# HGRN and Mamba mixers of a two-layer transformer step: the order of projections and small products on TensorE

## The chip, the cores and the metric

One core of one Trainium2 chip. The metric is the device time in microseconds of one execution of the whole kernel. The engines are TensorE (PE; its weight loads are listed as PEld), VectorE (DVE), ScalarE (ACT), GpSimd (POOL) and SyncE (SP). The profile counts microseconds from the start of its span.

## The reference

The model runs two layers on a prompt of 512 tokens and on 8 sampled tokens with states of their own. Each layer has a feed-forward block, a mixer and another feed-forward block. Only the mixer of the first layer matters here. Its input `h` is projected once, and then two things are computed side by side:

```python
proj = h @ P['w_in_ab']
q_a, f_a, i_a, g_a, z_b, xbc, dt_raw = jnp.split(...)
# HGRN2, 8 heads of 128: S_t = diag(f_t) S_{t-1} + k_t v_t^T,  o_t = S_t^T q_t
log_f = jnp.log(lb + (1 - lb) * jax.nn.sigmoid(fr)); k_a = (1 - lb) * jax.nn.sigmoid(-fr)
o_a, hg_s = hgrn2_chunked(silu(q_a), k_a, i_a, log_f, hg_s0, HG_CHUNK)
o_a = rmsnorm(o_a, hg_norm) * silu(g_a)
# Mamba-2, 16 heads in 4 groups: S_t = exp(dt_t A) S_{t-1} + B_t (dt_t x_t)^T,  y_t = S_t^T C_t
xbc_c = silu(causal_conv4(xbc) + b)
y, ssm_s = ssd_chunked(xh, dt, a_neg, B, C, ssm_s0, SSM_CHUNK)
y = rmsnorm_by_group((y + D * xh) * silu(z_b))
out = concat([o_a, y]) @ P['w_out_ab']
```

## The kernel before, in words

Everything lies transposed, with features on the partitions and 520 tokens (512 and 8) along the free axis. A product with a 1024 x 128 block of weights ("projection") is done in three passes: the high part of the weights by the high part of the input, the bf16 weights by the input's rest, and the weights' rest by the bf16 input. Each pass has 16 matmuls of 260 columns (`product_by_pass`, L940). ACT cuts the high part and the bf16 part (`cut_parts`, L1616, L1617) and DVE cuts the rest (`hgrn_cut` L2381, `ssm_cut` L2371). Two buffers hold the parts, so that projection number g may be cut once number g - 2 is done (`part_done`). When both weights of a load are cut, DVE frees its half of the ring and SP starts the next load.

The stages run one after the other, with fences between them; each engine has its own hand-written program, and semaphores join them. PSUM has eight banks of 512 columns, and each projection takes two of them.

HGRN, one pass of the loop per head: four projections FORGET, QUERY, VALUE, GATE. PE (`head`, L1117) does VALUE into bank 6 and GATE into bank 4 at the head's start, once the head before is done (`h_done`), with the transposes of the values (L1127) ahead of GATE's last pass. Then come the attention blocks of 128 tokens: product 0 within chunks and seven level products (L1152) with decays for distances 64, 32, ... 1, in banks 0 and 1 alternately, each evicted by DVE (L2475 to L2488). The keys are transposed after product 1 (L1133). Then state products (L1159), the broadcast of the 8 sampled values (L1163), the next head's FORGET into bank 2, output products (L1175, L1177), one-column products of the sampled states (L1181), and the next head's QUERY into bank 0 with the sums of squares (L867) after its first pass. ACT (L1829 on) makes the silu of the queries, the exponentials of decays (L1826, L1828, seven L1831), copies the values (VF, L1833; then L1835 to L1837), makes the silu of the gate (L1839), cuts the next FORGET and QUERY, copies the keys (L1847), multiplies the samples' keys and values (L1808), makes the next forget gates (L1801, L1802), cuts VALUE, squares the output, takes the logarithm of the gates (L1814) and the inverse root (L1572, L1574). DVE (L2431 on) cuts GATE's rest, makes decay differences (L2435 to L2442), products with queries and keys (L2445 to L2454), cuts FORGET and QUERY, splits the sampled values into three bf16 parts (L2462 to L2467), evicts the levels (L2482, L2475, L2485), gathers them (L2488), updates the sampled states (L2494) and the chunk states (L2499, L2502), does the next head's gates and its scan (L2422, L2423, L2426), and applies norm and gate (L2509, L2513). POOL loads the sampled states after `h_done` and stores both kinds of states.

Mamba, one pass per group (PE from L1247): six projections, numbers 0 to 3 for x, B, C, which are convolved on DVE (L2563 to L2569) and get a silu on ACT (L1904), and 4 and 5 for the two halves of z (silu L1901, L1908). PE does numbers 2 to 5, then transposes (L1260 to L1264), the broadcast of cumulated decays (L1269), the products of C and B (L1275), the next group's number 0, the state products (L1282, which wait for DVE's weighted values, L2633), ten filling matmuls (L874), the sample broadcast (L1289), output products (L1299, L1301) once DVE has the chunk states (L2647), one-column products (L1306), and the next group's number 1 with the sums. DVE scales the sampled states by L2596 and turns the transposed x into weighted values from L2600 on.

## Time and profile before

| | us |
|---|---|
| median of 3 runs | 3025.14 (3020.88 to 3027.26) |
| the profiled execution, its own time | 3025.36 |
| its span | 3023.8 |
| PE busy | 2807.6 (93%) |
| DVE busy | 1406.4 (47%) |
| ACT busy | 1355.1 (45%) |
| HGRN stage | about 497 to 838 |
| Mamba stage | about 868 to 1119 |

The span is the profiled execution on the core; 1.6 us lie around it. Busy shares are means over stages. A busy PE is not PE at its peak, since matmuls overlap; the clock that a stretch was granted is given as a share of full speed (1.00 is 2.4 GHz, 0.50 is 1.2 GHz).

### The profile page before, as it was taken

How to read it: one execution, taken by the hardware profiler on the slowest of the kernel's cores; microseconds unless marked ns; L12 is line 12 of the kernel's file. 1: busy time of each engine (PE TensorE's matmuls, PEld its weight loads, DVE VectorE, ACT ScalarE, POOL GpSimd, SP SyncE). 2: the span in 40 equal slices, each digit the busy share in tenths (PEclk: the TensorE clock that was granted, in tenths of full speed). 3: DMA queues.
4: the chain of work that ended last, by engine and by line, in shares of the span. 5: the costliest groups of instructions: out<-in, count | busy, mean ns of one | idle time of the engine just before them, and what ended most of it. 6: DMA issues, size and time to landing. Idle time of an engine off the chain costs nothing.

```text
span 3023.8 us, 60783 instructions
## 1 busy us (share of the span) xinstructions
PE 2807.6 (93%) x24504; PEld 2354.1 (78%) x24504; DVE 1406.4 (47%) x2893; ACT 1355.1 (45%) x2099; POOL 45.1 (1%) x78
## 2 busy tenths in 40 slices
PE   6999997887888989999999999999989989999997
PEld 3899885777667868799888899888856557789996
DVE  2444327666657763634425444333433434544433
ACT  3444337666643444634345434344423334544443
POOL 0000000000000000000000000000000000000000
PEclk8999998989999989999999999999999999999998
DMA  6223442121212224222343123432365435322221
GB/s 241 84 97 123 161 148 86 71 85 64 78 68 89 88 94 184 89 83 95 138 177 117 70 97 123 166 143 79 128 187 161 148 112 191 123 74 94 102 96 67
DMA packets 58281, 349.35 MB, mean 116 GB/s; under 512 B 7537, under 2 KB 7874, under 8 KB 28578
## 3 DMA queue, kind: packets, MB, share of 16 engines
q1 hardware_dynamic: 52274, 322.85, 30.0%
q0 software_dynamic: 5872, 24.59, 2.3%
q8 instruction: 98, 1.61, 0.2%
q14 instruction: 37, 0.30, 0.0%
HBM read 334.96 MB, written 12.45 MB: 115 GB/s over the span
## 4 chain that ended last, share of the span: by engine, by line
PE 76%; DVE 8%; ACT 8%; issue 3%; DVEq 2%; DMA 2%; ACTq 0%; PEldq 0%; SPq 0%; POOL 0%; PEld 0%
PE PS L940 54%; PE PS L918 2%; PE PS L954 2%; PE PS L867 2%; PE PS L1436 1%; PE PS L978 1%; PE PS L1418 1%; PE PS L1421 1%; PE PS L874 1%; PE PS L1397 1%; ACT hgrn_w_hi L1616 1%; DMA weight_ring<-in_mla_pairs 1%; PE PS L899 1%; ACT sub_out L1831 1%; PE PS L962 1%
## 5 line engine op out<-in xcount | busy, mean ns | idle before, releaser
L2167 DVE TENSOR_TENSOR w_rest<-weight_ring,w_hi 128x1024 bf16<-128x1024 f32 (+1 forms) x268 | 320.8, 1197 | 857.4 <-ACT w_hi L1616 857.2
L1616 ACT ACTIVATE w_hi<-weight_ring 128x1024 fp32r<-128x1024 f32 (+1 forms) x284 | 294.8, 1038 | 889.1 <-PE PS L940 886.0
L940 PE MATMUL PS<-hid_hi,w_hi 128*128 128x260 f32 x2432 | 326.9, 286 | 0.0
L940 PEld LDWEIGHTS PS<-hid_hi,w_hi 128*128 128x128 f32 x2432 | 299.2, 188 | 2.3
L940 PE MATMUL PS<-hid_rest,w_bf 128*128 128x260 bf16 x2432 | 298.4, 274 | 0.0
L940 PE MATMUL PS<-hid_bf,w_rest 128*128 128x260 bf16 x2432 | 296.7, 274 | 0.0
L1617 ACT ACTIVATE w_bf<-weight_ring 128x1024 bf16<-128x1024 f32 (+1 forms) x284 | 289.7, 1020 | 0.0
L940 PEld LDWEIGHTS PS<-hid_bf,w_rest 128*128 128x128 bf16 x2432 | 235.6, 97 | 36.5
L940 PEld LDWEIGHTS PS<-hid_rest,w_bf 128*128 128x128 bf16 x2432 | 223.9, 97 | 38.6
L940 PE MATMUL PS<-gu_hi,w_hi 128*128 128x260 f32 x1232 | 168.7, 288 | 0.0
L940 PEld LDWEIGHTS PS<-gu_hi,w_hi 128*128 128x128 f32 x1232 | 152.8, 188 | 14.1 <-issue 11.2
L940 PE MATMUL PS<-gu_rest,w_bf 128*128 128x260 bf16 x1232 | 152.3, 274 | 0.0
L940 PE MATMUL PS<-gu_bf,w_rest 128*128 128x260 bf16 x1232 | 151.3, 273 | 0.0
L940 PEld LDWEIGHTS PS<-gu_bf,w_rest 128*128 128x128 bf16 x1232 | 119.1, 97 | 18.6
L940 PE MATMUL PS<-hgrn_in_rest,hgrn_w_bf 128*128 128x260 bf16 x1056 | 133.0, 276 | 0.0
L940 PE MATMUL PS<-hgrn_in_bf,hgrn_w_rest 128*128 128x260 bf16 x1056 | 130.7, 274 | 0.0
L940 PE MATMUL PS<-mixer_in_hi,hgrn_w_hi 128*128 128x260 f32 x864 | 122.7, 297 | 6.3 <-ACT hgrn_w_hi L1616 5.1
L940 PEld LDWEIGHTS PS<-gu_rest,w_bf 128*128 128x128 bf16 x1232 | 112.8, 97 | 19.7
L940 PEld LDWEIGHTS PS<-mixer_in_hi,hgrn_w_hi 128*128 128x128 f32 x864 | 112.3, 198 | 9.7 <-ACT hgrn_w_hi L1616 5.4
L940 PEld LDWEIGHTS PS<-hgrn_in_bf,hgrn_w_rest 128*128 128x128 bf16 x1056 | 102.3, 97 | 16.2
L940 PEld LDWEIGHTS PS<-hgrn_in_rest,hgrn_w_bf 128*128 128x128 bf16 x1056 | 97.5, 98 | 18.7
L874 PE MATMUL PS<-consts 128*128 128x512 bf16 x337 | 86.6, 414 | 2.9 <-DVEq L558 2.9
(487 smaller groups left out, 4471.8 us busy)
## 6 DMA issues: line engine op xcount, KB each, us to landing
weight_ring<-in_ffn_gu SPq DMA_DIRECT2D x88, 1024.0 KB, 4.8
ada_chunks<-in_ada_w SPq DMA_DIRECT2D x40, 1536.0 KB, 6.6
weight_ring<-in_ffn_wd SPq DMA_DIRECT2D x32, 1408.0 KB, 6.0
weight_ring<-in_w_hgrn SPq DMA_DIRECT2D x16, 1024.0 KB, 4.8
weight_ring<-in_ada_w SPq DMA_DIRECT2D x8, 1536.0 KB, 7.2
weight_ring<-in_w_ssm SPq DMA_DIRECT2D x8, 1536.0 KB, 6.9
weight_ring<-in_mla_pairs SPq DMA_DIRECT2D x8, 1536.0 KB, 6.5
weight_ring<-in_w_out_ab SPq DMA_DIRECT2D x8, 1024.0 KB, 7.9
```

Of the source, the lines that this page charges most:

```text
L867: last = pe.matmul(PS[0:rows, bank + hf, 0:HT], weights[k], moving[k][:, hf * HT:(hf + 1) * HT], start=(k == 0), stop=(k == n - 1))
L874: pe.matmul(PS[:, bank, :], STEADY[:, 0:P], STEADY[:, 0:4 * P], start=True, stop=True)
L899: last = pe.matmul(PS[:, bank, 0:HT], w[:, k * P:(k + 1) * P], x[:, k, side(hf)], start=start and w is w_hi, stop=stop and w is w_rest)
L918: last = pe.matmul(PS[:, bank, 0:HT], w[:, k * P:(k + 1) * P], x[:, first + k, side(hf)], start=start and w is w_hi and k == 0, stop=stop ...
L940: last = pe.matmul(PS[:, bank + hf, 0:HT], w[:, k * P:(k + 1) * P], x[:, first + k, hf * HT:(hf + 1) * HT], start=start and w is w_hi and ...
L954: last = pe.matmul(PS[q * QR_:(q + 1) * QR_, 4, 0:3 * P], CS[:, k, :], weights[:, k * 3 * P:(k + 1) * 3 * P], start=(k < 4), stop=(k >= 4))
L962: last = pe.matmul(PS[:, 5, c * NSEQ:(c + 1) * NSEQ], MS[:, c * P:(c + 1) * P], const("fold")[:, 0:NSEQ], start=True, stop=True)
L978: last = pe.matmul(PS[:, 7, 0:HT], ONES, Y[:, c, side(hf)], start=(c == 0), stop=(c == DC - 1))
L1397: last = pe.matmul(PS[:, 4, :], WF[:, first:first + P], CKV[:, k, 0:NP_], start=(k == 0), stop=(k == RC - 1))
L1616: act.activation(hi, src, ACT.Copy).then_inc(w_hi_ready, 1)
L1617: act.activation(bf, src, ACT.Copy).then_inc(w_bf_ready, 1)
L2167: tt(WL_[:, buf, 0:n], W[:, slot, j * DC * P:j * DC * P + n], WH[:, buf, 0:n].bitcast(F32), ALU.subtract).then_inc(w_rest_ready, 1)
```

## The change

In HGRN the next head's four projections are spread over this head: FORGET after the key transposes (which come after all levels), QUERY after the sample broadcast, VALUE with the sums in it and GATE with the value transposes in it after the one-column products. VALUE now uses bank 2. On DVE the evictions of the levels come before the cuts of FORGET and QUERY and the splitting of the sampled values; the state update comes behind the next head's gates, so that the samples' gates and keys are copied first (FS, KS). ACT's program follows. In Mamba the second z half moves behind the products of C and B into bank 4; ACT copies it between the second and third segment exponential and makes its silu later. The diff, cut where "..." stands:

```diff
--- before.py
+++ after.py
@@ -285,6 +285,7 @@
         VM = yar.take(P // 2, rows=NB).bitcast(BF16)
+        FS, KS = yar.take(NB), yar.take(NB)
         S0 = ar.take(NB, P)
@@ -468,6 +469,7 @@
         g_z = sem("g_z")
+        g_zraw = sem("g_zraw")
         g_sel = sem("g_sel")
@@ -682,7 +684,7 @@
         QBANK, QTILE = (6, 2, 0), (0, 2 * 4, 4)
-        XBANK, ZBANK = (4, 2, 0, 6), (2, 0)
+        XBANK, ZBANK = (4, 2, 0, 6), (2, 4)
 
@@ -1115,27 +1117,26 @@
             def hgrn():
-                def project(h, c, bank, between=None, late=False):
-                    product_by_pass(hgrn_group(h, c), bank, c % 2, DC, 0, GHH, GHB, GHL, True, True,
+                def project(h, c, bank, between=None, late=False, ahead=0):
+                    product_by_pass(hgrn_group(h, c) + 4 * ahead, bank, c % 2, DC, 0, GHH, GHB, GHL, True, True,
                                     (GWH, GWB, GWL), between, late).then_inc(part_done, 1)
 
+                def values_and_gate(h, ahead, sums=None):
+
+                    def values_by_token():
+                        pe.wait_ge(h_vf, h + ahead + 1)
+                        for c in range(NCH):
+                            pe.transpose(PS[:, 2, c * P:(c + 1) * P], VF[:, c * CH:(c + 1) * CH], IDENT)
+                        pe.transpose(PS[0:NB, 3, 0:P], VF[:, NP_:T], IDENT).then_inc(h_vt, 1)
+
+                    pe.wait_ge(h_exp, h * 3 + (3 * ahead + 1))
+                    project(h, VALUE, 2, sums, False, ahead)
+                    if ahead:
+                        pe.wait_ge(h_r, h + 1)
+                    project(h, GATE, 4, values_by_token, True, ahead)
+
                 def head(h, more):
 
-                    def values_by_token():
-                        pe.wait_ge(h_vf, h + 1)
-                        for c in range(NCH):
-                            pe.transpose(PS[:, 6, c * P:(c + 1) * P], VF[:, c * CH:(c + 1) * CH], IDENT)
-                        pe.transpose(PS[0:NB, 7, 0:P], VF[:, NP_:T], IDENT).then_inc(h_vt, 1)
-
-                    def keys_by_token():
-                        pe.wait_ge(h_exp, h * 3 + 3)
-                        for c in range(NCH):
-                            last = pe.transpose(PS[:, 4, c * P:(c + 1) * P], KD[:, c * CH:(c + 1) * CH], IDENT)
-                        last.then_inc(h_kt, 1)
-
-                    pe.wait_ge(h_done, h + 1)
-                    project(h, VALUE, 6)
-                    project(h, GATE, 4, values_by_token, True)
                     pe.wait_ge(h_kd, h + 1)
@@ -1152,21 +1153,30 @@
                         last.then_inc(h_p, 1)
-                        if n == 1:
-                            keys_by_token()
+                    pe.wait_ge(h_exp, h * 3 + 3)
+                    for c in range(NCH):
+                        last = pe.transpose(PS[:, 4, c * P:(c + 1) * P], KD[:, c * CH:(c + 1) * CH], IDENT)
+                    last.then_inc(h_kt, 1)
+                    pe.wait_ge(h_v, h + 1)
+                    if more:
+                        project(h, FORGET, 2, None, False, 1)
+                    else:
+                        keep_busy(2, 12)
                     pe.wait_ge(h_kdt, h + 1)
...
                     pe.wait_ge(h_vs, h + 1)
+                    pe.wait_ge(h_done, h + 1)
                     for b in range(NB):
...
                     if more:
-                        project(h + 1, FORGET, 2)
+                        pe.wait_ge(h_ptk, h * 8 + 10)
+                        project(h, QUERY, 0, None, False, 1)
                     else:
-                        keep_busy(2, 30)
+                        keep_busy(2, 24)
                     pe.wait_ge(h_vk, h + 1)
@@ -1187,7 +1197,7 @@
                     if more:
-                        project(h + 1, QUERY, 0, sums)
+                        values_and_gate(h, 1, sums)
                     else:
@@ -1216,6 +1226,7 @@
                 pe.wait_ge(vec_in, 64)
+                values_and_gate(0, 0)
                 with pe.Fori(0, HG - 1) as h:
@@ -1249,9 +1260,8 @@
                     project(g, 3, XBANK[3])
-                    for c in range(2):
-                        pe.wait_ge(g_raw, g * 4 + (c + 2))
-                        project(g, 4 + c, ZBANK[c])
+                    pe.wait_ge(g_raw, g * 4 + 2)
+                    project(g, 4, ZBANK[0])
 
@@ -1264,7 +1274,7 @@
                     pe.wait_ge(g_sel, g + 1)
-                    pe.wait_ge(g_z, g * 2 + 2)
+                    pe.wait_ge(g_z, g * 2 + 1)
                     for j in range(GH):
@@ -1274,8 +1284,10 @@
                     last.then_inc(g_cb, 1)
-                    if more:
-                        pe.wait_ge(g_xd, g + 1)
+                    pe.wait_ge(g_xd, g + 1)
+                    project(g, 5, ZBANK[1])
+                    if more:
+                        pe.wait_ge(g_zraw, g + 1)
                         project(g + 1, 0, XBANK[0])
@@ -1806,7 +1818,7 @@
                         last = act.activation(VK[:, b, :], PS[:, 6 + b // 4, (b % 4) * P:(b % 4 + 1) * P],
-                                              ACT.Identity, scale=KK[:, NP_ + b:NP_ + b + 1])
+                                              ACT.Identity, scale=KS[:, b:b + 1])
                     last.then_inc(h_vk, 1)
@@ -1816,9 +1828,9 @@
                 forget_log(0)
+                cut(0, GATE)
 
                 def head(h, more):
-                    cut(h, GATE)
                     projected(h, QUERY)
@@ -1830,34 +1842,38 @@
                     projected(h, VALUE)
-                    act.activation(two(VF), pair(6), ACT.Copy).then_inc(h_vf, 1)
+                    act.activation(two(VF), pair(2), ACT.Copy).then_inc(h_vf, 1)
+                    if more:
+                        cut(h, FORGET, 1)
+                    else:
+                        ssm_cut(0, 0)
                     act.wait_ge(h_vt, h + 1)
-                    act.activation(VS, PS[0:NB, 7, 0:P], ACT.Copy)
-                    act.activation(V3[0:NB], PS[0:NB, 7, 0:P], ACT.Copy)
-                    act.activation(VV.rearrange("p a b -> p (a b)"), PS[:, 6, :], ACT.Copy).then_inc(h_v, 1)
+                    act.activation(VS, PS[0:NB, 3, 0:P], ACT.Copy)
+                    act.activation(V3[0:NB], PS[0:NB, 3, 0:P], ACT.Copy)
+                    act.activation(VV.rearrange("p a b -> p (a b)"), PS[:, 2, :], ACT.Copy).then_inc(h_v, 1)
                     projected(h, GATE)
+                    act.wait_ge(h_done, h + 1)
                     act.activation(two(GS), pair(4), ACT.Silu).then_inc(h_exp, 1)
                     if more:
-                        cut(h, FORGET, 1)
+                        act.preload_act_table_set("sigmoid_and_others")
                         cut(h, QUERY, 1)
                     else:
-                        ssm_cut(0, 0)
                         ssm_cut(0, 1)
...
                     if more:
-                        act.preload_act_table_set("sigmoid_and_others")
-                    sample_products(h)
-                    if more:
                         forget_gates(h, 1)
                         cut(h, VALUE, 1)
+                    else:
+                        both_tables()
+                    sample_products(h)
+                    if more:
+                        forget_log(h, 1)
                     act.wait_ge(h_o, h * 2 + 2)
...
                     if more:
-                        forget_log(h, 1)
-                    else:
-                        both_tables()
+                        cut(h, GATE, 1)
                     act.wait_ge(h_ss, h + 1)
@@ -1904,15 +1920,11 @@
                         ssm_cut(g, 0, 1)
-                    projected(g, 5)
-                    act.activation(two(GZ[:, 1, :]), pair(ZBANK[1]), ACT.Silu).then_inc(g_z, 1)
                     act.wait_ge(g_tr, g + 1)
...
                         act.activation(CEX[:, j, :], PS[:, j, :], ACT.Exp).then_inc(g_bcx, 1)
-                    if more:
-                        ssm_cut(g, 1, 1)
                     act.wait_ge(g_wl, g + 1)
@@ -1920,6 +1932,13 @@
                         act.activation(SEG[:, j, :], SEG[:, j, :], ACT.Exp).then_inc(g_sege, 1)
+                        if j == 1:
+                            projected(g, 5)
+                            act.activation(two(GZ[:, 1, :]), pair(ZBANK[1]), ACT.Copy).then_inc(g_zraw, 1)
+                    if more:
+                        ssm_cut(g, 1, 1)
+                    act.drain()
+                    act.activation(GZ[:, 1, :], GZ[:, 1, :], ACT.Silu).then_inc(g_z, 1)
                     if more:
@@ -2452,21 +2471,6 @@
                         tt(d[:, :, 0, :], d[:, :, 0, :], k[:, :, 0, :], ALU.mult).then_inc(h_qk, 1)
-                    if more:
-                        cut(h, FORGET, 1)
-                        cut(h, QUERY, 1)
-                    else:
-                        ssm_cut(0, 0)
-                        ssm_cut(0, 1)
-                    dve.wait_ge(h_v, h + 1)
-                    tt(VR, VS, V3[0:NB], ALU.subtract)
-                    dve.drain()
-                    dve.tensor_copy(VM, VR)
-                    dve.drain()
-                    tt(V3[64:64 + NB], VR, VM, ALU.subtract)
-                    dve.tensor_copy(V3[32:32 + NB], VM)
-                    dve.drain().then_inc(h_vs, 1)
-
                     for n in range(1 + len(LEVELS)):
@@ -2487,12 +2491,24 @@
                     dve.drain().then_inc(h_att, 1)
-
-                    dve.wait_ge(s_loaded, h * 16 + 16)
-                    dve.wait_ge(h_vk, h + 1)
-                    for b in range(NB):
-                        last = stt(S0[:, b, :], S0[:, b, :], FG[:, NP_ + b:NP_ + b + 1], VK[:, b, :], ALU.mult, ALU.add)
-                    last.then_inc(s_new, 1)
+                    if more:
+                        cut(h, FORGET, 1)
+                    else:
+                        ssm_cut(0, 0)
+                    dve.wait_ge(h_v, h + 1)
+                    tt(VR, VS, V3[0:NB], ALU.subtract)
+                    dve.drain()
+                    dve.tensor_copy(VM, VR)
+                    dve.drain()
+                    tt(V3[64:64 + NB], VR, VM, ALU.subtract)
+                    dve.tensor_copy(V3[32:32 + NB], VM)
+                    dve.tensor_copy(KS, KK[:, NP_:T])
+                    dve.drain().then_inc(h_vs, 1)
+                    if more:
+                        cut(h, QUERY, 1)
+                    else:
+                        ssm_cut(0, 1)
+
 
@@ -2502,8 +2518,17 @@
                     dve.drain().then_inc(h_s, 1)
-                    if more:
+                    dve.wait_ge(s_loaded, h * 16 + 16)
+                    if more:
+                        dve.tensor_copy(FS, FG[:, NP_:T])
                         forget(h, 1)
+                    else:
+                        dve.tensor_copy(FS, FG[:, NP_:T])
+                        dve.drain()
+                    dve.wait_ge(h_vk, h + 1)
+                    for b in range(NB):
+                        last = stt(S0[:, b, :], S0[:, b, :], FS[:, b:b + 1], VK[:, b, :], ALU.mult, ALU.add)
+                    last.then_inc(s_new, 1)
 
@@ -2661,6 +2686,7 @@
                     dve.drain()
+                    dve.wait_ge(g_z, g * 2 + 2)
                     tt(EV[:, 0:2, :], EV[:, 0:2, :], GZ, ALU.mult)
```

## Rows read from the trace of the kernel before

**Rows 1.** Windows, both stages: us, busy PE, PEld, DVE, ACT, POOL, clock, DMA share, GB/s.

```profile
497.00:838.00 341.00, 277.96 (x3679) 243.71 (x3680) 224.50 (x573) 220.93 (x350) 13.30 (x23) 0.90 0.21 74
868.00:1119.00 251.00, 223.69 (x1694) 187.50 (x1692) 190.29 (x424) 109.93 (x154) 17.09 (x27) 0.93 0.25 89
```

**Rows 2.** Waits, HGRN stage (497 to 838): us in total, times, longest.

```profile
PE PS L1152 <- DVE weight_parts L2482: 43.3, 8, 5.7
...
PE PS L1127 <- ACT arena L1833: 9.9, 8, 1.4
```

**Rows 3.** Timeline, PE in HGRN heads: start, us, engine, line, instructions, idle before.

```profile
534.50 0.65 PE L1175 MATMUL PS<-arena 128*128 128x128 f32 x4
...
746.17 0.68 PE L1175 MATMUL PS<-arena 128*128 128x128 f32 x4 [0.59 <-DVEq L2504]
...
747.80 1.84 PE L1181 MATMUL PS<-arena 128*128 128x1 f32 x16
...
749.51 2.16 PE L940 MATMUL PS<-mixer_in_hi,hgrn_w_hi 128*128 128x260 f32 x16
...
751.51 1.04 PE L867 MATMUL PS<-arena,consts 128*128 128x260 f32 x4
...
755.96 2.17 PE L940 MATMUL PS<-mixer_in_hi,hgrn_w_hi 128*128 128x260 f32 x16
...
761.48 2.17 PE L940 MATMUL PS<-mixer_in_hi,hgrn_w_hi 128*128 128x260 f32 x16
...
776.50 3.75 PE L1152 MATMUL PS<-sub_out 128*32 128x32 f32 x176 [5.44 <-DVE weight_parts L2482]
...
789.04 0.68 PE L1175 MATMUL PS<-arena 128*128 128x128 f32 x4 [0.60 <-DVEq L2504]
```

**Rows 4.** Timeline, DVE in the HGRN head of 746 to 789.

```profile
754.02 0.69 DVE L2509 TENSOR_TENSOR inv_rms<-inv_rms,PS 128x512 f32<-128x512 f32 x1 [1.66 <-ACT inv_rms L1574]
...
757.26 1.23 DVE L2381 TENSOR_TENSOR hgrn_w_rest<-weight_ring,hgrn_w_hi 128x1024 bf16<-128x1024 f32 x1 [0.71 <-ACT hgrn_w_hi L1616]
...
758.69 0.69 DVE L2435 TENSOR_TENSOR arena<-arena 128x512 f32<-128x512 f32 x1 [0.21 <-issue]
...
764.01 0.68 DVE L2445 TENSOR_TENSOR arena<-arena 128x512 f32<-128x512 f32 x1
...
776.16 0.29 DVE L2482 TENSOR_TENSOR weight_parts<-PS,consts 128x128 f32<-128x128 f32 x1 [0.20 <-issue]
```

**Rows 5.** Groups by line, ACT, same head: xcount, busy us, mean ns, idle.

```profile
L1616 ACT ACTIVATE hgrn_w_hi<-weight_ring 128x1024 fp32r<-128x1024 f32 x4 | 4.2, 1052 | 2.2 <-PE PS L940 2.2
...
L1808 ACT ACTIVATE arena<-PS,arena 128x128 f32<-128x128 f32 x8 | 2.2, 384 | 7.0 <-PE PS L1163 7.0
...
L1849 ACT ACT_TABLE_LOAD x1 | 1.3, 1283 | 0.0
```

**Rows 6.** Windows around falls of the clock; columns as in the first group.

```profile
966.00:971.00 5.00, 4.89 (x15) 2.96 (x16) 4.88 (x10) 2.83 (x3) 0.00 (x0) 0.66 0.00 0
775.00:783.00 8.00, 6.33 (x194) 5.81 (x195) 4.46 (x17) 1.00 (x2) 0.00 (x0) 0.57 0.53 197
2226.50:2228.70 2.20, 0.03 (x1) 0.00 (x0) 1.88 (x10) 0.81 (x4) 0.00 (x0) 1.00 0.85 250
2229.00:2234.00 5.00, 5.00 (x17) 2.36 (x16) 1.02 (x5) 2.84 (x9) 0.00 (x0) 0.66 0.85 250
```

**Rows 7.** Waits, Mamba stage (868 to 1119).

```profile
PE PS L1282 <- DVEq L2634: 21.7, 4, 8.8
...
PE PS L1299 <- DVEq L2648: 5.2, 3, 1.7
```

**Rows 8.** Timeline, second Mamba group, ACT and DVE around the transposes.

```profile
947.73 2.21 ACT L1904 ACTIVATE arena<-arena 128x520 f32<-128x520 f32 x4
...
948.50 2.50 DVE L2596 TENSOR_TENSOR sub_out<-sub_out,arena 128x512 f32<-128x512 f32 x4 [0.20 <-issue]
...
954.28 1.29 DVE L2600 TENSOR_TENSOR arena<-PS,arena 128x512 f32<-128x512 f32 x2 [3.28 <-PE PS L1264]
```

4 lines of the change are left out of this document (2 added, 2 removed).

## The prediction

> **What bounds the kernel now.** The windows of the two stages that the change touches come first. In 341 us of HGRN, TensorE (PE) is busy 278, VectorE (DVE) 224 and ScalarE (ACT) 221; in 251 us of Mamba PE has 224, DVE 190, ACT 110 [rows 1]. So PE has 63 and 27 us of gaps, the most that new order alone could win without the clock, which is 0.90 and 0.93 of full here. The waits say where they are: 43.3 us in eight pieces where the level products wait for DVE's first eviction, and 21.7 and 5.2 us in Mamba where PE waits for DVE's weighted values and states [rows 2, 7]. No engine is full. Each head is a loop of waits through three engines, and its period is what counts: from the first output product of the first head (534.50) to that of the seventh (789.04), six periods, 42.4 us each [rows 3].
>
> **HGRN, the new loop at full clock.** PE does the same four projections per head, about 5.5 us each (755.96 to 761.48) [rows 3], so nothing is removed; I follow the wait that ends last around one head.
>
> 1. From the inverse root on DVE: norm, gate and the rest cut end at the decay differences, 4.7 us from 754.02 to 758.69, of which 1.3 was a wait for GATE's cut that ACT now makes before: 3.4. Key decay and differences take 5.3 (to 764.01) [rows 4], the decay products 5.9 (estimate: 764.01 plus the same 14 pairs and two products). Evictions now follow at once instead of at 776.16; PE ends the last level product 2.9 later (estimate from the 3.75 us that levels 2 to 7 took at half clock). Sum 17.5.
> 2. Key transposes 0.5 and FORGET 5.5: 6.0. They were behind the second level and at the end.
> 3. ACT takes two sigmoids (1.05), a table load 1.28, VALUE's cut of two passes (1.05 each, of which 0.1 overlaps), eight sample products 2.1 [rows 5] and a logarithm 0.6: 6.95. DVE then scans (1.3) and updates the sampled states (2.2) before PE may use them: 10.5 in all. Beside it PE has state products 1.0, sample broadcast 0.7, QUERY 5.5 and output products 1.8 (746.17 to the next line's work), 9.0: it waits 1.5.
> 4. One-column products 1.7, VALUE's high pass 2.0, sums 0.9, inverse root 1.4: 6.0 [rows 3].
>
> The sum is 40.0, against 42.4: **2.4 us less per head** before the clock. Inside step 1 PE runs 7.3 us of VALUE and GATE after the sums, while VF is copied only behind nine exponentials (1.4 + 3.4 + 5.3 + 1.1 = 11.2): a **new wait of 4 us** before GATE's last pass; behind it are the value transposes and all levels. It replaces the 5.4 us wait at 776.50.
>
> **The clock.** After 5.4 us of waiting the clock was 0.57 over 8 us, that is, half for 6.9 us; the Mamba wait of 4.3 us was followed by 0.66 over 5 us, half for 3.4; and a gap of 2.2 us late in the kernel also by 0.66 over 5 us [rows 3, 6, 7]. The old wait of 1.4 us for the values [rows 2] and 1.7 us of one-column products left it full. The new head has two stretches of the falling kind: 1.5 + 1.7 = 3.2 us of waiting and one-column products, and the 4 us. The first puts VALUE's high pass and the sums, 2.9 us on the path, partly at half: +1.2. The second slows the value transposes, GATE's last pass and first levels by 2.3 to 3, of which 1.7 is slack since PE would wait for DVE after the second level: +0.8. Together +2.0, hence 42.0 per head, **0.4 less** than now.
> The Trainium skill, page "TensorE: Matmul & The Clock Gate", section "HAM oscillation — how this bites in real kernels", says that waits between short bursts of products throttle PE again and again, and that work should be arranged so that PE stays busy. It speaks against this spreading, which makes two such stretches of one; by it both falls come in every head, as taken above; without it the head would be 40.0.
>
> **HGRN, sum.** Six periods give 6 x 0.4 = 2.4 and the last head 0.5. The first head gains more, 3: its levels no longer stand behind the two weight cuts and the value parts on DVE (about 6), but QUERY (5.5) now comes before the output, and a half clock of 6.9 us (about 2.5 of loss) is gone. **-6.**
>
> Costed at nothing: the copies of KK and FG samples (8 columns, DVE idles 6 us in each head by this plan); the FORGET and QUERY cuts on ACT moved before the key copy (that copy is needed only after 5.5 us of FORGET; without this cover they cost 1.9 each). The state load on the POOL queue still starts at the end of the head before; DVE now waits for it ahead of the next gates, about 24 us later. A transfer that late would hold the gates, the VALUE cut and the scan queued behind it. The GATE silu now also waits for the previous head's end, 10 us earlier than ACT gets there. SP's weight loads hang on the same rest cuts, in the same order.
>
> **Mamba.** One projection (z1, 5.5 us) leaves the place before the transposes. It does not give 5.5: ACT has z0's silu first and then the conv silus from 947.73 at 0.55 each, three of which PE needs, so 949.4; transposes 1.5 gives 950.95, and DVE is in the state scaling to 951.0 anyway. DVE's chain starts at 951.05 instead of 954.28 [rows 8]: **3.2 earlier**, and all behind it (cuts, segment sums, weighted values, states, 20 us without a stall) follows. z1 ends near 958.9; ACT copies it between two segment exponentials, releases bank 4 at 960.4, and the next group's projection ends at 965.9. The state products wait for that, no longer for DVE, and end 0.2 before DVE needs them. The extra silu (0.6) and its table load (1.3 [rows 5]) lie in ACT's idle time: it is busy 110 of 251 us [rows 1]. Without that cover they are 1.9 per group. What is late next is DVE itself. The clock takes something back: the new 2.4 us gap before the transposes is as long as the late gap of [rows 6]; cold transposes and broadcasts cost 0.8. Three groups at -2.4, and the last -4.3, as its 8.8 us wait [rows 7] shrinks to about 3 and less of its fill runs at half clock: **-11.5.** The bounds: 0 if the slack of 0.2 fails and the states come 3.2 late again; -15 if the clock holds.
>
> **Sum.** -6 - 11.5 = -17.5 on the profiled execution's own 3025.36, 3007.9; it lies 0.2 above the median, so **3008**.
>
> **Rivals.**
> - *The new stretches leave the clock full.* For it: the longest is 4.0, below the 5.4 at which HGRN's clock falls now. Against: 4.3 and 2.2 were enough elsewhere [rows 6, 7]. HGRN gains 6 x 2.4 + 0.5 + 3 = 18, Mamba 15: 2992.
> - *Mamba gives nothing.* z1 runs at half clock behind the gap, its copy holds two segment exponentials and bank 4, the state products come 3 us later and the gain is used up: HGRN's 6 and 2 for the last group, 3017. For it is the slack of 0.2; against it that the gap is short and one projection is long.
> - *Slower.* The level products (32 columns each) now stand alone between GATE and FORGET with no projection among them. If their sparse 5 us also bring the clock down, the key transposes and FORGET run at half for up to 6.9 us, on the path: +2.8 at least on 42.0, 44.8 and 2.4 x 8 = 19 more than now; less Mamba's 11.5 this is 3033. It decides the sign once half clock costs above 3.8 per head (2.4 plus 11.5 / 8) instead of 2.0. For it: the clock stayed low through these products in the old head [rows 6]. Against: there it had fallen before.
>
> **Chances.** Forecast 0.5, full clock 0.2, Mamba nothing 0.22, slower 0.08. The range runs from the second case (2992) to just above the third: 3022. A measurement can tell 0.2% (6 us) from no change: faster means below 3019. All of the first two cases and half of the third are faster, 0.81; same 0.11; slower 0.08.
>
> **What would show it.** Right: first output products 42 us apart, PE waiting about 4 us for VF inside GATE and 1.5 before the one-column products, two falls of the clock per head, the wait before the level evictions gone; in Mamba the transposes 3 us earlier against the group's start, no wait of 4.3 us before the state products, groups near 59.3. Wrong: one fall or none per head (faster), a third (slower), a wait for DVE's weighted values still there, or ACT idling behind z1.

## The result and the profile after

The change made the kernel 0.2% slower. Median of 11 runs 3032.15 us (3028.74 to 3035.77), against 3027.26 us (3020.88 to 3032.67, 11 runs) for the kernel before on the same chip: ratio 1.0021, 95% interval 1.0011 to 1.0030. The profiled execution took 3032.8 (span 3031.2). I had forecast 3008 and a range from 2992 to 3022.

| read from the two traces | before | after | difference |
|---|---|---|---|
| first output product of the first head | 534.50 | 533.22 | -1.3 |
| the six periods to that of the seventh head, mean | 42.42 | 44.53 | +2.1 each, +12.7 |
| last norm-and-gate (end of HGRN) | 838.65 | 849.40 | +10.75 |
| from there to the first product of the down stage behind Mamba | 284.87 | 281.63 | -3.2 |
| from there to the end | 1900.3 | 1900.2 | -0.1 |

So the whole loss is in the six periods of HGRN's loop, and Mamba gives a quarter of it back. The stages in windows, columns as in [rows 1]:

```profile
497.00:838.00 341.00, 283.20 (x3625) 245.19 (x3626) 222.59 (x577) 225.10 (x345) 11.49 (x21) 0.88 0.20 72
868.00:1119.00 251.00, 227.56 (x1710) 190.96 (x1709) 194.92 (x435) 117.19 (x164) 17.10 (x27) 0.91 0.26 90
```

TensorE (PE) is busy for longer, 283 for 278 in HGRN [rows 1], and that is no work: the window holds fewer products (3625 for 3679), at a lower clock (0.88 for 0.90, and 0.91 for 0.93 in Mamba). The waits of the kernel after, in us in total, times, longest:

```profile
PE PS L1129 <- ACT arena L1845: 33.5, 8, 4.8
PE PS L1191 <- DVE arena L2530: 15.4, 7, 2.2
...
PE PS L1270 <- ACT arena L1920: 9.3, 4, 2.3
PE PS L942 <- ACT arena L1937: 5.0, 3, 1.8
...
PE PS L1294 <- DVEq L2659: 2.7, 1, 2.7
```

The 43.3 us in front of the level evictions [rows 2] are gone. In their place stand 33.5 where the value transposes wait for the copied values, and 15.4 where the one-column products wait for VectorE's (DVE's) update of the sampled states. In Mamba the 21.7 us of L1282 [rows 7] have shrunk to 2.7, and 9.3 before the transposes and 5.0 for the bank of z1 are new. One head of the kernel after on PE:

```profile
756.32 0.61 PE L1185 MATMUL PS<-arena 128*128 128x128 f32 x4
...
760.24 1.95 PE L1191 MATMUL PS<-arena 128*128 128x1 f32 x16 [2.19 <-DVE arena L2530]
762.05 3.17 PE L942 MATMUL PS<-mixer_in_hi,hgrn_w_hi 128*128 128x260 f32 x16
765.01 1.65 PE L869 MATMUL PS<-arena,consts 128*128 128x260 f32 x4
...
778.67 1.11 PE L1129 MATMUL PS<-consts,arena 128*128 128x128 f32 x4 [4.71 <-ACT arena L1845]
...
779.79 3.66 PE L942 MATMUL PS<-hgrn_in_bf,hgrn_w_rest 128*128 128x260 bf16 x16
...
783.77 3.81 PE L1153 MATMUL PS<-sub_out 128*64 128x64 f32 x184
787.51 0.66 PE L1158 MATMUL PS<-consts,arena 128*128 128x128 f32 x4
787.93 2.17 PE L942 MATMUL PS<-mixer_in_hi,hgrn_w_hi 128*128 128x260 f32 x16
...
800.43 0.61 PE L1185 MATMUL PS<-arena 128*128 128x128 f32 x4
```

Both waits are where the prediction put them. Behind each, PE falls to half clock (a "fall" from here on): VALUE's high pass takes 3.17 (2.16 at full), the sums 1.65 (1.04 at full), GATE's last pass 3.66 (1.95 at full). Every head of the loop has both falls. This one is of the commoner kind; in two of the six periods the first fall is longer (VALUE's high pass 3.81 and 3.60) and the period is 45.5 and 45.0 instead of 44.1 to 44.2. The key transposes and FORGET run at full clock again. On DVE in the same head:

```profile
756.65 1.23 DVE L2445 TENSOR_TENSOR_SCAN arena<-mixer_consts,arena 128x512 f32<-128x512 f32 x1 [1.84 <-ACT arena L1826]
757.99 2.19 DVE L2530 SCALAR_TENSOR_TENSOR arena<-arena,sub_out 128x128 f32<-128x128 f32 x8
768.13 0.69 DVE L2534 TENSOR_TENSOR inv_rms<-inv_rms,PS 128x512 f32<-128x512 f32 x1 [7.95 <-ACT inv_rms L1586]
...
772.06 0.69 DVE L2454 TENSOR_TENSOR arena<-arena 128x512 f32<-128x512 f32 x1 [0.20 <-issue]
...
783.92 0.29 DVE L2486 TENSOR_TENSOR weight_parts<-PS,consts 128x128 f32<-128x128 f32 x1 [0.55 <-PE PS L1153]
```

DVE idles 1.84 for the logarithm, scans, updates the sampled states, and then idles 7.95 for the inverse root. So the update stands in the short piece of DVE's work for which PE waits, and 8 us of idle time follow it. The experiments test that place.

### The profile page after: what moved, and what is told of

The parts are those of the page before. It is cut to its first block, busy times and chain, and to the rows that moved or that the text cites. A ratio compares the mean times of both kernels' runs of the same rounds, so it can differ in the third digit from the quotient of the medians.

```text
span 3031.2 us, 60863 instructions
## 1 busy us (share of the span) xinstructions
PE 2829.4 (93%) x24510; PEld 2368.9 (78%) x24510; DVE 1408.2 (46%) x2909; ACT 1368.5 (45%) x2107; POOL 44.4 (1%) x78
## 4 chain that ended last, share of the span: by engine, by line
PE 78%; DVE 9%; ACT 6%; issue 3%; DVEq 2%; DMA 1%; ACTq 0%; PEldq 0%; SPq 0%; POOL 0%; PEld 0%
PE PS L942 55%; PE PS L920 3%; PE PS L956 2%; PE PS L869 2%; PE PS L980 1%; PE PS L1448 1%; PE PS L1430 1%; PE PS L901 1%; PE PS L1433 1%; PE PS L1344 1%; PE PS L964 1%; PE PS L1409 1%; PE PS L876 1%; DVE arena L2771 1%; PE PS L1440 1%
## 5 line engine op out<-in xcount | busy, mean ns | idle before, releaser
L942 PE MATMUL PS<-hgrn_in_bf,hgrn_w_rest 128*128 128x260 bf16 x1056 | 142.3, 289 | 0.0
L942 PE MATMUL PS<-mixer_in_hi,hgrn_w_hi 128*128 128x260 f32 x864 | 130.6, 309 | 11.9 <-ACT hgrn_w_hi L1628 5.2
L942 PEld LDWEIGHTS PS<-gu_bf,w_rest 128*128 128x128 bf16 x1232 | 119.2, 97 | 18.6
L942 PEld LDWEIGHTS PS<-mixer_in_hi,hgrn_w_hi 128*128 128x128 f32 x864 | 119.9, 210 | 15.5 <-issue 13.9
L942 PEld LDWEIGHTS PS<-hgrn_in_bf,hgrn_w_rest 128*128 128x128 bf16 x1056 | 108.3, 103 | 21.9
```

Source lines behind the costliest of these rows:

```text
L942: last = pe.matmul(PS[:, bank + hf, 0:HT], w[:, k * P:(k + 1) * P], x[:, first + k, hf * HT:(hf + 1) * HT], start=start and w is w_hi and ...
```

## The experiments

Two theories. **Order and clock:** the new loop of waits is itself hardly shorter than the old one, and its two stretches at half clock per head cost the rest. **Loop alone:** the period is set by ScalarE (ACT) and DVE, and the clock is beside the path. The head's period is the mean of the six between first output products, "last gate" the last norm-and-gate, Mamba the stretch of the table above, rest what follows it. Each ratio is to the kernel before on the same chip; the runs are from several chips, so two runs are compared by their ratios where their medians are close.

| run | median us | ratio to before, 95% | period | last gate | Mamba | rest |
|---|---|---|---|---|---|---|
| after | 3032.15 | 1.0021 (1.0011 to 1.0030) | 44.5 | 849.4 | 281.6 | 1900.2 |
| hgrn_only | 3043.64 | 1.0049 (1.0035 to 1.0062) | 44.5 | 850.6 | 285.3 | 1907.2 |
| mamba_only | 3022.10 | 0.9979 (0.9970 to 0.9988) | 42.6 | 839.5 | 279.0 | 1896.3 |
| fill_values | 3038.88 | 1.0032 (1.0022 to 1.0042) | 45.1 | 854.3 | 281.5 | 1898.9 |
| fill_both | 3019.66 | 0.9972 (0.9961 to 0.9982) | 42.6 | 841.7 | 279.6 | 1899.0 |
| before_fill | 3024.04 | 0.9987 (0.9978 to 0.9996) | 41.2 | 836.0 | 285.3 | 1903.3 |
| s0_early | 3009.45 | 0.9937 (0.9925 to 0.9950) | 41.0 | 825.9 | 281.5 | 1900.9 |
| vf_early | 3040.14 | 1.0042 (1.0029 to 1.0055) | 45.8 | 863.9 | 280.0 | 1902.5 |
| s0_fill | 3013.11 | 0.9947 (0.9934 to 0.9960) | 41.9 | 834.1 | 279.6 | 1903.3 |
| s0_vf_fill | 3012.76 | 0.9952 (0.9937 to 0.9967) | 40.7 | 831.6 | 280.0 | 1899.0 |
| s0_mfill | 3001.40 | 0.9918 (0.9905 to 0.9931) | 41.1 | 822.7 | 274.2 | 1899.0 |
| s0_zearly | 3008.75 | 0.9936 (0.9924 to 0.9948) | 40.9 | 828.3 | 277.3 | 1898.8 |
| s0_both_m | 3003.30 | 0.9927 (0.9915 to 0.9939) | 41.1 | 825.9 | 273.3 | 1903.1 |

The last column is the same code in every kernel and yet lies between 1896.3 and 1907.2. So spans of single executions are not compared below a dozen us; the stages are, and the medians of several runs.

**The two parts alone.** hgrn_only is the kernel before with every edit of the diff in HGRN, mamba_only with every edit in Mamba.

> The kernel before with the HGRN part of the change alone; Mamba is as before. By the two traces HGRN's end (the last norm-and-gate) moved from 838.65 to 849.40, so the HGRN part alone should cost +10.8: 3036 against a median of 3025 to 3027 before (ratio 1.0036), with a head period of 44.2 and two stretches at half clock per head. If instead the two parts meet (the last head's cuts and Mamba's first group share the weight buffers), the sum of the two parts alone differs from the whole by more than 1.

> The kernel before with the Mamba part alone. By the two traces the stretch from the last norm-and-gate to the end of the Mamba stage got 3.2 shorter, so this alone should give -3.2 against the kernel before (ratio 0.9989); my forecast had put -11.5 on it. If the part is worth nothing by itself and the 3.2 came from a start that HGRN's end left differently, it gives 0; if the forecast's working was right and HGRN's late end spoilt it, -8 to -11.

HGRN alone has the period of the whole change (44.5), and Mamba alone gains 5.9 in its own stretch (279.0 against 284.9). That is more than the 3.2 expected and less than 8: 3.7 of it lie before the last group's output products and 2.2 behind them, in products that no edit touches and that met full clock here (21.9 for 24.1). The product of the two ratios is 1.0028, inside the interval of the whole: no sign that the parts meet. hgrn_only's 16 us in the median are more than the 12.0 of its last gate; its interval begins at 10.6, and the 6.9 of the rest column is code that I did not change.

**Idle products in the waits.** They put work for PE where it waits anyhow.

```diff
                     def values_by_token():
+                        if ahead:
+                            pe.wait_ge(h_exp, h * 3 + 5)
+                            keep_busy(0, 18)
                         pe.wait_ge(h_vf, h + ahead + 1)
```

```diff
+                    if more:                      # fill_both only
+                        pe.wait_ge(h_exp, h * 3 + 4)
+                        keep_busy(2, 9)
                     pe.wait_ge(s_new, h + 1)
```

> The kernel after with 18 idle products of 512 columns (0.216 each warm, 3.9 in all) on TensorE's free bank 0 before the wait for the copied values inside GATE's projection (4.7 long at present), in the seven heads of the loop. They delay nothing: the wait stays, only TensorE is busy in it. Clock theory: the second stretch at half clock of each head (6.8 long, over GATE's rest, the level products and the key transposes) goes, and the head's period falls from 44.1 by 1.5 to 2.5, to some 42; total 3032 - 7x2 = 3018. Rival (the period is set by the loop of waits through ScalarE and VectorE, whose work isn't clocked by TensorE's gate): the period stays at 44.1 and the time at 3032.

> As the run before it, and 9 more idle products before the wait for the sample states' update (2.2 long, between the output products and their one-column products). Clock theory: the first stretch at half clock (over the products of VALUE's hi part) goes as well, another 1.5 per head; period 40.5, the loop that I had summed without any clock term (40.0); total near 3006. Rival (loop of waits without clock): 3032 again, the idle products change nothing.

fill_values met neither expectation: period and last gate are worse than in the kernel after (45.1 for 44.5, 854.3 for 849.4), and so is the median (3038.88 for 3032.15), though the two intervals just overlap. In three of the six heads the second fall is gone and in three it comes later, behind the level products; the first fall got longer in five. A head of fill_values on PE:

```profile
763.33 2.32 PE L1194 MATMUL PS<-arena 128*128 128x1 f32 x16 [2.19 <-DVE arena L2533]
765.51 3.81 PE L942 MATMUL PS<-mixer_in_hi,hgrn_w_hi 128*128 128x260 f32 x16
769.12 1.94 PE L869 MATMUL PS<-arena,consts 128*128 128x260 f32 x4
...
783.65 1.95 PE L942 MATMUL PS<-hgrn_in_bf,hgrn_w_rest 128*128 128x260 bf16 x16
...
788.01 3.63 PE L1156 MATMUL PS<-sub_out 128*32 128x32 f32 x176 [1.41 <-DVE weight_parts L2489]
```

GATE's last pass is at full clock (1.95) as wished, but VALUE's high pass is now slow from end to end (3.81), and the inverse root hangs on it: from the one-column products to the root this head takes 9.2, the kernel after mostly 7.9. With both waits filled, some heads have no fall at all. One of them, at a granted clock of 1.00 from 664.5 to 706.5:

```profile
664.68 0.61 PE L1188 MATMUL PS<-arena 128*128 128x128 f32 x4
...
668.59 1.95 PE L1197 MATMUL PS<-arena 128*128 128x1 f32 x16 [0.24 <-DVE arena L2536]
670.40 2.16 PE L942 MATMUL PS<-mixer_in_hi,hgrn_w_hi 128*128 128x260 f32 x16
...
685.46 0.66 PE L1132 MATMUL PS<-consts,arena 128*128 128x128 f32 x4 [0.84 <-ACT arena L1851]
...
693.55 0.66 PE L1161 MATMUL PS<-consts,arena 128*128 128x128 f32 x4
...
706.47 0.61 PE L1188 MATMUL PS<-arena 128*128 128x128 f32 x4
```

PE still waits 0.24 and 0.84 behind the idle products, so they delay nothing. The period is 41.8, not 40.5. (Three of the six heads are like this; the others have one or two falls and take 43.0 to 43.7, hence the total of 3019.66 and not 3006.) So the clock costs 44.1 - 41.8 = 2.3 in a head of the commoner kind and 44.5 - 41.8 = 2.8 in the mean, and the loop alone is 41.8, 1.8 above my 40.0. Both theories hold a part of the loss.

**The same clock in the old order.** 22 idle products behind the key transposes of the kernel before.

```diff
                         if n == 1:
                             keys_by_token()
+                            keep_busy(2, 22)
```

> The kernel before with 22 idle products (4.75) in front of its wait for the first level eviction (5.4), behind the key transposes. It asks what the same clock is worth in the old order. Clock theory: its one stretch at half clock of each head goes, level products 3 to 7 and part of FORGET run at full speed; the first take about 3.75 at half, but VectorE's evictions (0.58 each, 3.5 for the last six) set them anyway, so the gain is what FORGET and the transposes lose, 1 to 2 per head: 40.5 to 41.5, total 3011 to 3019. That would be below the 41.8 of the new order without a fall: then the new order has no gain of its own. If half clock is hidden behind VectorE in the old order: 42.4, 3026.

```profile
700.91 0.68 PE L1176 MATMUL PS<-arena 128*128 128x128 f32 x4 [0.59 <-DVEq L2505]
...
731.25 3.20 PE L1152 MATMUL PS<-sub_out 128*32 128x32 f32 x176 [0.69 <-DVE weight_parts L2483]
...
742.14 0.68 PE L1176 MATMUL PS<-arena 128*128 128x128 f32 x4 [0.59 <-DVEq L2505]
```

The period is 41.2 in all six, the clock 1.00, and PE still waits 0.69 behind the idle products. The total missed its expectation (3024 for 3011 to 3019): the first output product came 1.5 later, the last head took 44.0 for 41.9, and the rest column is 3 above that of before. But the loop says what was asked: **at full clock the old order takes 41.2 and the new one 41.8**. As it stands, the new order has no gain of its own.

**Where the order loses it.** In the kernel before, DVE updated the sampled states ahead of the state products; the change moved the update behind the next head's gates and the scan. s0_early puts it before the wait for the logarithm; vf_early copies the values earlier, in ACT's order; s0_fill is s0_early with the 18 idle products of fill_values.

```diff
                     cut(h, VALUE, ahead)
+                    if samples:
+                        samples()          # wait for VK, eight updates of S0
                     dve.wait_ge(h_lf, h + (ahead + 1))
                     dve.tensor_tensor_scan(BB, const("reset"), EB, 0.0, ALU.mult, ALU.add)
```

```diff
                     act.activation(EB, BB, ACT.Exp).then_inc(h_ex, 1)
+                    projected(h, VALUE)                                      # vf_early
+                    act.activation(two(VF), pair(2), ACT.Copy).then_inc(h_vf, 1)
```

> The kernel after, with VectorE's update of the sampled states (2.2) put in front of its wait for the logarithm instead of behind the scan. VectorE idles 1.8 there and 6 behind, so nothing else on it gets late, and TensorE's one-column products can start about 2 earlier. It takes 2 out of the loop of waits, and with it most of the idle time that comes before the first stretch at half clock. Loop theory, corrected by the last runs (41.8 without clock, 2.3 for the clock): -1.9 to -2.2 for the wait and up to -1 if the first fall goes too, so 44.1 becomes 41 to 42.2, over eight heads -15 to -24, 3008 to 3017. Rival (the wait before the one-column products isn't on the path, VectorE's chain to the level evictions is): 0, since VectorE has the same work in the same head.

> The kernel after, with ScalarE's copy of the values right behind the first exponential (where ScalarE idles 0.8) instead of behind all nine, so that the wait of 4.7 inside GATE's projection is gone. By the after trace VectorE's decay products, not TensorE, are what the first level eviction waits for (TensorE is 0.5 late there at half clock), so the wait only moves to the place before the level products: idle 4 to 6 there again, 'wait for VectorE's first eviction' as in the kernel before; period 43.5 to 44.1, total -4 to 0 (3028 to 3032). Rival (the wait for the values that I had forecast as a cost of the change is what made it slower): -4 per head, 3000.

> The update of the sampled states in front of the scan and, besides, the 18 idle products before the wait for the values. By the two runs with idle products: without any fall in a head the loop was 41.8; with the update early it should be 39.8, the first time that the order of the change shows a gain: 3032 - 8 x 4.3 = 2998 if no fall is left, 3005 if one of 3.4 is left per head. If VectorE's own chain sets the loop: 3019, as with both fills.

s0_early is 22.7 us faster than the kernel after (ratios 0.9937 and 1.0021, intervals far apart) and 0.63% faster than the one before; its last gate is 23.5 earlier than that of the kernel after. DVE and PE in one of its heads:

```profile
657.09 2.19 DVE L2528 SCALAR_TENSOR_TENSOR arena<-arena,sub_out 128x128 f32<-128x128 f32 x8 [1.31 <-ACT arena L1820]
659.21 1.22 DVE L2447 TENSOR_TENSOR_SCAN arena<-mixer_consts,arena 128x512 f32<-128x512 f32 x1
665.65 0.69 DVE L2539 TENSOR_TENSOR inv_rms<-inv_rms,PS 128x512 f32<-128x512 f32 x1 [5.24 <-ACT inv_rms L1586]
```

```profile
657.29 0.61 PE L1185 MATMUL PS<-arena 128*128 128x128 f32 x4
...
659.34 1.95 PE L1191 MATMUL PS<-arena 128*128 128x1 f32 x16 [0.33 <-DVE arena L2528]
661.15 2.16 PE L942 MATMUL PS<-mixer_in_hi,hgrn_w_hi 128*128 128x260 f32 x16
...
676.19 1.11 PE L1129 MATMUL PS<-consts,arena 128*128 128x128 f32 x4 [4.71 <-ACT arena L1845]
```

The wait is 0.33 for 2.19, VALUE's high pass is at full clock here, the scan now ends with 5.24 us to spare. The wait of 4.71 for the values and the fall behind it are still there; they cost 0.9 (the table of the loop's parts). vf_early takes that wait away and becomes slower, which neither theory had expected. PE in one of its heads:

```profile
790.54 0.46 PE L1153 MATMUL PS<-arena 128*32 128x32 f32 x32 [2.50 <-DVE arena L2466]
...
795.36 3.75 PE L1153 MATMUL PS<-sub_out 128*32 128x32 f32 x176 [3.04 <-DVE weight_parts L2486]
799.04 1.12 PE L1158 MATMUL PS<-consts,arena 128*128 128x128 f32 x4
799.81 2.92 PE L942 MATMUL PS<-mixer_in_hi,hgrn_w_hi 128*128 128x260 f32 x16
```

PE now waits 2.50 before the first level product and 3.04 before the third, and the key transposes (1.12 for 0.66) and FORGET's start (2.92 for 2.17), which stand on the path, are slow behind them. The wait for the values, which I had called a cost of the change, is only the place where PE waits for DVE's products. s0_fill missed (3013 for 2998 to 3005): with one wait filled, five of the six periods have a fall over VALUE's high pass, where s0_early has two, and four have one over the key transposes (up to 1.12).

**No fall and no wait.** s0_vf_fill is s0_early and vf_early with idle products where PE then waits.

```diff
+                    pe.wait_ge(h_exp, h * 3 + 2)
+                    keep_busy(0, 10)
                     pe.wait_ge(h_kd, h + 1)
                     for n in range(1 + len(LEVELS)):
+                        if n == 2:
+                            pe.wait_ge(h_done, h + 1)
+                            keep_busy(6, 14)
```

> The kernel with the early update of the sampled states, with the values' copy behind the first exponential (so no wait in GATE) and idle products where TensorE then waits: 10 before the first level product, 14 before the third. TensorE is at full clock in the loop as far as this reaches. By the sum corrected with measured terms: 4.0 + 5.3 + 5.9 + 3.5 to the key transposes, 6.0 for these and FORGET, 8.9 to the one-column products, 6.3 to the next root: 39.9 against 40.7, over eight heads -6, 3003. If the falls only move, as with the fill before the wait for the values: 41 to 42, 3010 to 3018.

Heads without a fall take 39.9, as summed; three of the six do, the others 41.5. In the total the second case of the expectation came (3013, no better than s0_early's 3009): besides those falls, the first output product comes 3.8 later than in s0_early (538.0 for 534.2) and the stretch from the seventh head's to the last gate is 3.9 longer (49.4 for 45.5). The fall in those three comes behind the same work. Two neighbouring heads of this one run:

```profile
661.45 1.95 PE L1196 MATMUL PS<-arena 128*128 128x1 f32 x16 [0.33 <-DVE arena L2533]
663.25 3.69 PE L942 MATMUL PS<-mixer_in_hi,hgrn_w_hi 128*128 128x260 f32 x16
...
702.90 1.95 PE L1196 MATMUL PS<-arena 128*128 128x1 f32 x16 [0.33 <-DVE arena L2533]
704.71 2.16 PE L942 MATMUL PS<-mixer_in_hi,hgrn_w_hi 128*128 128x260 f32 x16
```

The loop in its three parts, from the timelines of one head each (us):

| part | forecast | after | fill_both | s0_early | s0_vf_fill |
|---|---|---|---|---|---|
| inverse root to key transposes | 17.5 | 19.4 | 18.7 | 19.6 | 18.6 |
| key transposes to one-column products | 16.5 | 16.8 | 16.8 | 15.0 | 15.0 |
| one-column products to inverse root | 6.0 | 7.9 | 6.3 | 6.3 | 6.3 |
| period | 40.0, with clock 42.0 | 44.1 | 41.8 | 40.8 | 39.9 |

**Mamba.** On top of s0_early: 10 idle products before the transposes (s0_mfill), the z1 copy one exponential earlier (s0_zearly), and both (s0_both_m).

```diff
-                    pe.wait_ge(g_x, g * 4 + 3)
                     pe.wait_ge(g_raw, g * 4 + 4)
+                    keep_busy(0, 10)
+                    pe.wait_ge(g_x, g * 4 + 3)
```

```diff
-                        if j == 1:
+                        if j == 0:
                             projected(g, 5)
```

> The kernel with the early update of the sampled states (3009.5), and in each Mamba group 10 idle products (2.2) on the free bank 0 in front of the wait for ScalarE's conv silus (2.3 long). Clock theory for the Mamba part's missing gain (I had forecast -11.5, alone it gave -5.9): the transposes run at half clock behind that wait (2.9 instead of 1.5), and so does part of the projection before the state products, which makes these late for VectorE. With the wait filled: -1.4 for the transposes and up to -1 for the states per group, -5 to -9 in all, 3001 to 3005. Rival (the gain is lost in the order of ScalarE's work: the z1 copy behind two segment exponentials holds the bank 1.8): 0, 3009.

> The kernel with the early update of the sampled states, and ScalarE's copy of z1 behind the first segment exponential instead of the second: 0.94 earlier by the trace (948.97 against 948.03), so the projection that waits for its bank starts 0.9 earlier in three groups. By the order theory -0.9 each, 3 less, 3006.5, if the state products are on the path; by the clock theory the gap before it gets shorter and may keep the clock, 1 more each. If VectorE is the chain in that place: 0.

> The update of the sampled states early, the idle products before Mamba's transposes, and the z1 copy behind the first segment exponential: the three edits that helped or did no harm, together. By the traces Mamba (last HGRN gate to the first product of its heads) takes 284.9 in the kernel before, 281.6 after, 278.6 with the idle products and 277.3 with the early copy. If the two add up: 275 to 276, and 2998 to 3000 in all. If they take the same gap (the state products of each group need only one of the two): 277 to 278.5 and 3001, as with the idle products alone.

The second group of the kernel after on PE, around the wait for the silus and the wait for z1's bank, and then the second wait in s0_mfill, with its first product of the down stage:

```profile
960.64 0.57 PE L1270 MATMUL PS<-consts,arena 128*128 128x128 f32 x2 [2.34 <-ACT arena L1920]
...
965.57 2.17 PE L942 MATMUL PS<-mixer_in_hi,hgrn_w_hi 128*128 128x260 f32 x16
...
973.14 2.77 PE L942 MATMUL PS<-mixer_in_hi,hgrn_w_hi 128*128 128x260 f32 x16 [1.80 <-ACT arena L1937]
975.71 3.01 PE L942 MATMUL PS<-hgrn_in_rest,hgrn_w_bf 128*128 128x260 bf16 x16
...
980.35 1.89 PE L1294 MATMUL PS<-arena 128*128 128x256 f32 x8
```

```profile
945.01 2.17 PE L942 MATMUL PS<-mixer_in_hi,hgrn_w_hi 128*128 128x260 f32 x16 [1.55 <-ACT arena L1938]
947.02 1.96 PE L942 MATMUL PS<-hgrn_in_rest,hgrn_w_bf 128*128 128x260 bf16 x16
...
1096.91 0.48 PE L892 MATMUL PS<-heads_hi,w_hi 128*128 128x260 f32 x2 [2.06 <-ACT heads_bf L1775]
```

From the first transpose to z1's projection the kernel after takes 4.9 where the one before took 3.5 to its next projection, and the projection that the state products stand behind takes 1.65 longer (2.77 + 3.01 for 2.17 + 1.96). With the first wait filled this projection is at full clock, although the second wait is still there (1.55). The early copy shortens the wait for the bank from 5.0 to 2.3 us in total.

The Mamba stretch in two parts, with the last group's output products between them (us). The code of the second part is the same in all:

| | before | after | mamba_only | s0_early | s0_mfill | s0_zearly | s0_both_m |
|---|---|---|---|---|---|---|---|
| last gate to the last group's output products | 260.8 | 257.6 | 257.1 | 257.4 | 251.8 | 254.9 | 251.4 |
| from there to the down stage | 24.1 | 24.1 | 21.9 | 24.1 | 22.4 | 22.4 | 21.9 |

In the first part the filled wait gives 5.6 over s0_early, the early copy 2.5, and both 6.0. So **they don't add up; they mostly take the same time**. The expectation of s0_both_m names 278.6 for s0_mfill. That was read at a later product of the down stage; the first one stands at 1096.91, which gives 274.2. What is late next is DVE: with the early copy PE waits 4.1 us in total for it before the output products, and 3.9 with both edits, for 1.8 in s0_early. s0_mfill met its expectation (3001 to 3005), s0_zearly did not show its 3 us in the total. The totals agree with the stage: s0_both_m (0.9927) is not better than s0_mfill (0.9918), and s0_zearly (0.9936) is level with s0_early (0.9937), so the 2.5 of the early copy are seen in the stage alone, in one execution. s0_mfill beats both given kernels: 0.82% under the one before. Against s0_early the stage shows its gain; the intervals of the two ratios still overlap.

## Why the prediction was wrong

The forecast was 25 us too low for the profiled execution: 17 of them in HGRN (+10.75 for -6) and 8 in Mamba (-3.2 for -11.5).

**The step that failed is the sum of HGRN's loop at full clock: 40.0, "2.4 us less per head before the clock".** In a head without a fall the loop measured 41.8 (fill_both), only 0.6 under the old 42.4. The clock term, taken at 2.0, was 2.8 in the mean. Together the period is 44.5 for the 42.0 of the forecast, and the sign turns. In the terms of the prediction:

1. *Step 1*, taken at 17.5, measured 18.65. Norm, gate and cut to the differences took 3.9 for 3.4: the 1.3 that I took off as a wait for GATE's cut was 0.71 of wait [rows 4] and 0.59 of gap between two instructions, and the gap stays. The level evictions took 3.5 for 2.9, since DVE makes them one by one every 0.58. Step 2 was right (6.0). Step 3 was 10.8 for 10.5 (its terms for ACT add up to 7.03, not 6.95, which changes nothing), step 4 6.3 for 6.0. The errors have one sign, and a good part of them is gaps of 0.2 to 0.6 between dependent instructions.
2. *The 2.4 compared unlike loops.* The 40.0 was a loop at full clock, the 42.4 the old head with its fall in it [rows 3]. At full clock the old one is 41.2 (before_fill). The forecast of 42.0 against 42.4 had the falls on both sides, so this did not make the number wrong; it hid that the order was summed to be worth only 1.2, less than its error.
3. *The update of the sampled states was counted on the path and not questioned.* Step 3 has it: "updates the sampled states (2.2) before PE may use them". Its cost was right; that the old place had been better was overlooked. It is the one edit whose undoing repays the loss: 1.9 less in step 3, and in the heads where the first fall goes with it 1.6 more. With the update early (and the values' copy too, in s0_vf_fill) the new order takes 39.9 at full clock against 41.2 of the old one: the rest of the reordering does have a gain.

**The clock was right in kind and too small in size.** There are two falls per head, at the two places named. In four of the six heads they cost 2.3 for the forecast 2.0, namely 1.6 (taken 1.2) over VALUE's high pass and the sums, and 0.7 (taken 0.8) in the levels. In the other two the first fall costs 3.1. The Trainium skill, page "TensorE: Matmul & The Clock Gate", section "HAM oscillation — how this bites in real kernels", says that waits which come back between short bursts of products throttle PE each time; the kernel after agrees, with two falls in every head and a granted clock of 0.88 in this stage for 0.90.

**The wait for the values** of 4 us came (4.7). By itself it costs nothing: step 1 takes 18.65 in a head without a fall, both with the copy as late as in the kernel after (fill_both) and with it early (s0_vf_fill). Only the fall behind the wait costs, 0.7 to 0.9.

**The first head** gained 1.3 for the 3 of the forecast, the last 0.6 for 0.5. HGRN: -1.3 + 6 x 2.1 - 0.6, against my -6.

**Mamba** gave -3.2 in the whole kernel, for -11.5. The transposes do come earlier, as taken: against the start of its group's first projection 3.0 in the second group (19.13 for 22.14). They stand behind 2.3 of waiting and no longer behind a projection of 5.6. What failed is the "slack of 0.2 at the state products". In the second group a projection at half clock is 1.65 longer, ACT frees z1's bank behind two exponentials (1.8 of waiting), and DVE waits 1.7 for the states. From the last gate to each group's output products the change gives -1.5, +2.1, -2.7 and -1.1 for the groups in turn. In the third group the clock stayed at 1.00 from before the transposes to the output products (1010 to 1045), DVE did not wait for the states, and the group took 59.0, near the forecast 59.3: so the sum of this step was right where the clock stayed full there. This is the second rival's mechanism, in part. With both places mended Mamba gives -11.6 (273.3), the forecast's number; that is partly luck, since 2.2 of it come behind the last output products. The last group gave 1.1 for my 4.3.

**The rivals.** The slower one (3033) has the measured time and not the cause: the key transposes (0.66) and FORGET's high pass (2.17) after the level products are at full clock in every head of the kernel after's loop. Its mechanism does exist: in heads of fill_values, fill_both, s0_fill and vf_early the key transposes take up to 1.12 and FORGET's high pass up to 2.96, some of them with no fall earlier in the head. There the stretch from the key transposes to the one-column products is 1.0 longer (17.8 for 16.8 in vf_early), which is part of what vf_early and s0_fill lose. That the forecast gave the measured time only 0.08 has another reason: my slower case had one mechanism and no room for the loop's sum being off by 1.8, 14 us in eight heads.

## What to carry to other kernels

Before an order is costed, bring both loops to the same clock: take the old one's fall out as carefully as the new one's is put in, and add the small gaps between dependent instructions, which all point one way. When an edit moves work on an engine that idles, ask whether it lands before or behind the next thing that another engine waits for. Here 2.2 us of VectorE were put behind another wait although 8 us of idle time followed; PE got them 2 us late in each of eight heads, and with the falls that this brought it cost 23 us. Idle products in a wait have to be tried and then read in the trace: in HGRN one filled wait gave nothing or cost time (fill_values, s0_fill), both together gave 0.5% (1.0021 to 0.9972), and in Mamba one alone shortened the part with the groups by 5.6.

## What the hardware showed that I had not expected

- Filling one wait can lengthen the fall behind another: with the same products in front of it, VALUE's high pass took 2.80 to 3.81 in the heads of the kernel after and 3.45 to 3.82 in those of fill_values, and the median went from 3032.15 to 3038.88 (ratios 1.0021 and 1.0032, the intervals just overlap).
- The same work need not meet the same clock: in s0_vf_fill a wait of 0.33 and 1.95 of one-column products were followed by 3.69 in one head and by 2.16 in the next, periods 41.5 and 39.9. In the kernel after the same wait of 2.34 before Mamba's transposes was followed by half clock in the second group and by a clock of 1.00 in the third.
- The unchanged part of the kernel took between 1896.3 and 1907.2 in the fourteen single executions profiled.
